# Attention scores: the scale moved into the queries, the maxima written negated, the mask added to the outer key blocks alone

## The chip, the cores and the metric

The kernel runs on one core of one Trainium2 chip, as one launch. The metric is the time of an execution on the device in microseconds (us); a lower number is better. The engines are called by their roles: TensorE (PE in the profile, its weight loads PEld), VectorE (DVE), ScalarE (ACT), GpSimd (POOL), and SyncE (SP), which issues the DMAs.

## What the kernel computes

Two blocks in a row on 512 tokens of width 1024. The first block (a convolution and pooling mixer, then a layer of 16384 experts looked up by key, then a gated embedding) takes the first 1700 us or so and isn't touched. The second block has two attention layers. The first, "a", is a windowed attention with 16 query heads on 4 key heads; its core in the reference is:

```
q = apply_rope(q, cos, sin);  k = apply_rope(k, cos, sin)        # the 512 tokens; the 256 context tokens are not rotated
near = jnp.abs(kj - BLOCK - qi) <= WINDOW                        # previous, own and next block of 128 keys
s_loc = jnp.einsum("bqhgd,bkhd->bhgqk", q, k).astype(F32) * scale    # scale = 64 ** -0.5
s_loc = jnp.where(m, s_loc, -jnp.inf)
s_ctx = jnp.einsum("bqhgd,bchd->bhgqc", q, kc).astype(F32) * scale
p = softmax_with_sink(jnp.concatenate([s_loc, s_ctx], axis=-1), sink_b)
...
sc = jnp.einsum("bqhgd,bkhd->bhgqk", qc, kc).astype(F32) * scale     # queries of the context
```

The second, "b", is a latent attention of 16 heads, in which each of the 512 queries attends to all 768 keys:

```
q = (rms_norm_2(cq, q_norm) @ w_uq);  rope on 32 of its 96 columns
s = (einsum(qn, kn) + einsum(qr, kr)) * scale                     # scale = 96 ** -0.5
p = jax.nn.softmax(s, axis=-1)
```

## The kernel before

Every engine has one list of instructions, written out in order in the functions `tensor`, `scalar`, `vector`, `gpsimd` and `sync`. Nothing reorders them. An engine runs ahead until a `wait_ge` on a semaphore that another engine (or an earlier instruction of its own) raises with `then_inc(*tick(...))`.

**Layer a.** The eight query units are projected one after the other (`on_both`, some 9 us each on TensorE). ScalarE copies the 512 token columns of a unit out of PSUM (L1203), TensorE multiplies them with the rotation matrix (L607), and VectorE finishes the rotation in three instructions (`rope`, L1704 to L1706). The 256 context columns come as two partial sums that VectorE adds up (`context_sum`, L1711). Then come 96 jobs. Job j is one block of 128 queries of one head; `a_job(j)` gives the query unit i (0 to 7), the half (which of the unit's two heads) and the block t (0 to 3 are the tokens, 4 and 5 the context). The two halves of one (i, t) are called a pair of jobs here, and there are 48 pairs, six to a unit. A half has its own PSUM area, `SC[half]`, and there is one of each, so that the scores of a pair can start only when both exponentials of the pair before have been read. A pair goes so:

- TensorE, `a_scores`: scores against the 256 context keys (L696); for t below 4 against the 256 or 384 near keys too (L701), onto which the mask is added by a matmul of the identity with the mask's columns, in the rounded fp32 type (L704). The mask holds 0 or -1e30.
- VectorE, `maxima`: for t = 0 a copy of the sink value (L1745) into the score area, for every job the row maximum (L1746) and its product with -scale (L1747).
- ScalarE, `exponents`: the exponential (L1212), which reads the scores, scales them, adds the bias from L1747 and sums the row.
- VectorE, `normalise`: the reciprocal of the sum (L1752) and the product (L1753).
- TensorE, `a_turn`: transposes (L718); ScalarE copies them out of PSUM (L1230 to L1236); a unit later TensorE weighs the values with them (L745, L747, L752), and VectorE multiplies by the gate (L1768).

TensorE's order is: scores of the next pair, some pieces of the weighing of the unit before, the transposes of this pair. With t = 0 the unit before is gated.

**Layer b.** 64 jobs, one block of 128 queries of one head each, eight to a pair of heads. The order on TensorE is: transposes (L726), scores of the job after next (L877, L878), a step of the next head pair's projection (L843, L848, L857, the rotation L607), a piece of the weighing (L888). ScalarE copies the projected queries out (L1339). VectorE's order is: normalise, in two of eight jobs the three rotation instructions, then `maxima`.

`far_sink` holds the sinks divided by the scale, since the scores in PSUM are unscaled:

```
sc, sm = SC[j % 2], small[:, j % 16, :]
step(("max", key, j), DVE.tensor_reduce(sm[:, 0:1], sc[:, lo:hi], AX.X, ALU.max))
DVE.tensor_scalar(sm[:, 1:2], sm[:, 0:1], -scale, None, ALU.mult).then_inc(*tick("maxed", (key, j)))
```

`step` puts a wait of VectorE on its own instruction behind it.

Of the kernel before, what the change touches and what calls it, by code (L numbers as in the profile page):

```python
# [8 lines left out]
F32 = mybir.dt.float32  # L9
F32R = mybir.dt.float32r  # L10
U32 = mybir.dt.uint32
AF = mybir.ActivationFunctionType
AX = mybir.AxisListType

P = 128
T = 512
# [110 lines left out]
def write(nc, d, known):  # L127
# [37 lines left out]
    gathered = nc.alloc_sbuf_tensor("gathered", [P, T], F32)[:, :]  # L165
    fin_gain = nc.alloc_sbuf_tensor("fin_gain", [P, KC], F32)
    small = nc.alloc_sbuf_tensor("small", [P, 16, 8], F32)
    far_sink = nc.alloc_sbuf_tensor("far_sink", [P, 16], F32)
    psum = nc.alloc_psum_tensor("psum", [P, 8 * T], F32)
    bank = [psum[:, b * T:(b + 1) * T] for b in range(8)]  # L170

# [211 lines left out]
    def tensor(PE):  # L383
# [299 lines left out]
        def a_scores(j):  # L683
            i, _, t = a_job(j)
            p = i % 2
            lo, tiles = a_tiles(t)
            both = [(SC[half], slice(64 * half, 64 * half + 64)) for half in range(2)]
            if j:
                PE.wait_ge(*at("exped", ("a", j - 2)))
                PE.wait_ge(*at("exped", ("a", j - 1)))  # L690
            else:
                PE.wait_ge(*at("mask_r", 0))
                for n in range(8):
                    PE.wait_ge(*at("roped", ("q", n)))
            for sc, rows in both:
                last = PE.matmul(sc[:, T:TC], qr[i][rows, t * P:(t + 1) * P], kt[rows, p, T:TC], start=True, stop=True)  # L696
            if t < NT:
                first = tiles[0]
                skip = (first - t + 1) * P
                for sc, rows in both:  # L700
                    PE.matmul(sc[:, lo:T], qr[i][rows, t * P:(t + 1) * P], kt[rows, p, first * P:(tiles[-3] + 1) * P],  # L701
                              start=True, stop=False)
                for sc, rows in both:
                    last = PE.matmul(sc[:, lo:T], mask_r[:, 3 * P:4 * P], mask_r[:, skip:skip + T - lo], start=False,  # L704
                                     stop=True)
            last.then_inc(*tick("scored", ("a", j)))


# [216 lines left out]
    def scalar(ACT):  # L925
# [271 lines left out]
        for i in range(8):  # L1197
            u = unit("a_q", i)
            high_weights(u + 1)
            if i == 0:  # L1200
                a_silu_ctx(7)
            ACT.wait_ge(*at("unit", u))
            ACT.activation(qr[i][:, 0:T], bank[2 * (i % 4)], AF.Copy).then_inc(*tick("qr", i))  # L1203
        ACT.activation(mask_r[:, 3 * P:4 * P], K("ident"), AF.Copy)
        ACT.activation(mask_r[:, 0:3 * P], K("mask"), AF.Copy).then_inc(*tick("mask_r", 0))

        def exponents(key, j, probs, lo, hi, scale, turned):
            sm = small[:, j % 16, :]
            ACT.wait_ge(*at("maxed", (key, j)))
            if turned >= 0:  # L1210
                ACT.wait_ge(*at("prob_turned", (key, turned)))
            ACT.activation(probs[j % len(probs)][:, 0:hi - lo], SC[j % 2][:, lo:hi], AF.Exp, bias=sm[:, 1:2], scale=scale,  # L1212
                           accum_out=sm[:, 2:3]).then_inc(*tick("exped", (key, j)))

        def a_exponents(j):
            exponents("a", j, prob, a_tiles(a_job(j)[2])[0], SINK + 1, A_SCALE, j // 2 * 2 - 4)

        def a_turn(j):
            i, half, t = a_job(j)
# [107 lines left out]
        def project(pair, step):  # L1327
# [8 lines left out]
            elif step % 2 == 0:  # L1336
                i = step // 2 - 1
                ACT.wait_ge(*at("q_up", (pair, i)))
                ACT.activation(q[head_rows[i], i, :], bank[7][head_rows[i], :], AF.Copy).then_inc(*tick("qh", (pair, i)))  # L1339

        def b_exponents(j):
            exponents("b", j, b_prob, 0, TC, B_SCALE, j - PROBS)

        def b_turn(j):
            pair, half, t = b_job(j)
# [34 lines left out]
    def vector(DVE):  # L1380
# [296 lines left out]
        first = VEC["g_final"][0]  # L1677
        step("fin_gain", DVE.tensor_tensor(fin_gain[:, :], ada[:, 0, 1, :, 0], vec[:, first:first + KC], ALU.mult))
        sinks = vec[:, VEC["sink"][0]:VEC["sink"][0] + 16]
        step("far_sink", DVE.tensor_scalar(far_sink[:, :], sinks, 1.0 / A_SCALE, None, ALU.mult))  # L1680


        DVE.wait_ge(*at("peer_added", 7))
# [48 lines left out]
        for i in range(8):  # L1732
            u = unit("a_q", i)
            low_weights(u + 1)
            if i:
                a_rope(("q", i - 1), qr[i - 1], 2 * ((i - 1) % 4))
            context_sum(u, 2 * (i % 4) + 1, qr[i][:, T:TC]).then_inc(*tick("qr_ctx", i))
        a_rope(("q", 7), qr[7], 6)
        DVE.wait_ge(*at("a_silu_ctx", 7))

        def maxima(key, j, lo, hi, scale, sink=None, scored=None):
            sc, sm = SC[j % 2], small[:, j % 16, :]
            DVE.wait_ge(*at("scored", (key, j if scored is None else scored)))
            if sink is not None:
                step(("sunk", j), DVE.tensor_copy(sc[:, SINK:SINK + 1], far_sink[:, sink:sink + 1]))  # L1745
            step(("max", key, j), DVE.tensor_reduce(sm[:, 0:1], sc[:, lo:hi], AX.X, ALU.max))  # L1746
            DVE.tensor_scalar(sm[:, 1:2], sm[:, 0:1], -scale, None, ALU.mult).then_inc(*tick("maxed", (key, j)))  # L1747

        def normalise(key, j, probs, n):
            pr, sm = probs[j % len(probs)], small[:, j % 16, :]  # L1750
# [3 lines left out]

        def a_maxima(j):
            i, half, t = a_job(j)
            maxima("a", j, a_tiles(t)[0], SINK + 1, A_SCALE, (i // 2) * 4 + 2 * (i % 2) + half if t == 0 else None,
                   j // 2 * 2)

        def a_normalise(j):  # L1760
# [84 lines left out]
                norm("b_cq")  # L1845

        def b_maxima(j):
            maxima("b", j, 0, TC, B_SCALE)

        def b_normalise(j):  # L1850
            normalise("b", j, b_prob, TC)
# [354 lines left out]
```

## Time and profile before

| | |
|---|---|
| median of 3 runs | 2546.21 us |
| lowest and highest | 2545.77, 2550.89 us |
| profiled execution, its own time | 2547.82 us |
| profiled execution, span | 2546.5 us |
| TensorE busy | 2365.4 us, 93% |
| VectorE busy | 1867.6 us, 73% |
| ScalarE busy | 1074.8 us, 42% |
| layer a, the jobs | 1775 to 1990 us from the span's start |
| layer b, projections of the head pairs and the jobs | 2165 to 2485 us |

Busy shares are means over the whole span. The two stretches of the attention jobs are some 535 us of it, and what is worth something there is read from the chain of work in them. The profiled execution lies 1.3 us over its span and 1.6 us over the median.

### The profile page before, as it was taken

How to read it: one execution, taken by the hardware profiler on the slowest of the kernel's cores; microseconds unless marked ns; L12 is line 12 of the kernel's file. 1: busy time of each engine (PE TensorE's matmuls, PEld its weight loads, DVE VectorE, ACT ScalarE, POOL GpSimd, SP SyncE). 2: the span in 40 equal slices, each digit the busy share in tenths (PEclk: the TensorE clock that was granted, in tenths of full speed). 3: DMA queues.
4: the chain of work that ended last, by engine and by line, in shares of the span. 5: the costliest groups of instructions: out<-in, count | busy, mean ns of one | idle time of the engine just before them, and what ended most of it. 6: DMA issues, size and time to landing. Idle time of an engine off the chain costs nothing.

```text
span 2546.5 us, 33616 instructions
## 1 busy us (share of the span) xinstructions
PE 2365.4 (93%) x12399; PEld 1986.8 (78%) x12399; DVE 1867.6 (73%) x3575; ACT 1074.8 (42%) x1910; POOL 623.0 (24%) x408
## 2 busy tenths in 40 slices
PE   7989999999999989999999998998778989899997
PEld 5768998999899989999999986786444767455555
DVE  7899898999999977878788875524676454155554
ACT  3332333333488843333333344321566333344452
POOL 4110367777722232323233302000000100000001
PEclk9999999999999999999999999999899999999999
DMA  6537456787788999999999941111000112100001
GB/s 246 188 134 252 163 191 223 248 249 251 246 318 322 326 366 358 367 357 363 327 368 367 365 153 59 58 58 50 1 1 1 50 42 99 36 19 19 10 1 67
DMA packets 162227, 465.95 MB, mean 183 GB/s; under 512 B 15504, under 2 KB 72976, under 8 KB 159632
## 3 DMA queue, kind: packets, MB, share of 16 engines
q1 hardware_dynamic: 100368, 304.40, 34.1%
q0 software_dynamic: 36864, 134.23, 14.8%
q10 hardware_dynamic: 24832, 25.17, 3.0%
q8 instruction: 99, 1.62, 0.3%
q14 instruction: 64, 0.52, 0.1%
HBM read 411.31 MB, written 52.43 MB: 182 GB/s over the span
## 4 chain that ended last, share of the span: by engine, by line
PE 70%; DVE 17%; ACT 4%; DMA 4%; issue 3%; POOL 2%; DVEq 0%; ACTq 0%
PE psum L572 6%; PE psum L574 6%; PE psum L573 6%; PE psum L428 5%; PE psum L430 5%; PE psum L429 5%; PE psum L436 4%; PE psum L438 4%; PE psum L437 4%; PE psum L545 3%; PE psum L857 2%; DMA arena<-hidden 2%; PE psum L454 2%; POOL weights_low L1948 2%; DVE small L1746 2%
## 5 line engine op out<-in xcount | busy, mean ns | idle before, releaser
L934 ACT ACTIVATE weights_high<-arena 128x1024 fp32r<-128x1024 f32 x355 | 374.8, 1056 | 439.7 <-PE psum L574 303.6
L1387 DVE TENSOR_TENSOR weights_low<-arena,weights_high 128x1024 fp32r<-128x1024 f32 x266 | 334.6, 1258 | 217.7 <-ACT weights_high L934 208.8
L436 PE MATMUL psum<-x_high,weights_high 128*128 128x384 f32 x1024 | 352.3, 344 | 28.8 <-POOL weights_low L1948 19.5
L572 PE MATMUL psum<-hidden_high,weights_high 128*128 128x384 f32 x1024 | 344.9, 337 | 10.2 <-DVE hidden_low L1649 8.0
L438 PE MATMUL psum<-x_high,weights_low 128*128 128x384 f32 x1024 | 344.4, 336 | 0.0
L437 PE MATMUL psum<-x_low,weights_high 128*128 128x384 f32 x1024 | 344.2, 336 | 0.0
L573 PE MATMUL psum<-hidden_low,weights_high 128*128 128x384 f32 x1024 | 343.4, 335 | 0.0
L574 PE MATMUL psum<-hidden_high,weights_low 128*128 128x384 f32 x1024 | 343.2, 335 | 0.0
L428 PE MATMUL psum<-x_high,weights_high 128*128 128x512 f32 (+1 forms) x696 | 277.1, 398 | 24.7 <-DVE weights_low L1387 19.9
L1948 POOL TENSOR_TENSOR weights_low<-arena,weights_high 128x1024 fp32r<-128x1024 f32 x89 | 227.1, 2552 | 201.3 <-ACT weights_high L934 200.8
L429 PE MATMUL psum<-x_low,weights_high 128*128 128x512 f32 (+1 forms) x696 | 271.7, 390 | 0.0
L430 PE MATMUL psum<-x_high,weights_low 128*128 128x512 f32 (+1 forms) x696 | 271.6, 390 | 0.0
L1942 POOL DMA_INDIRECT arena<-in_v_rows,arena x128 | 152.4, 1191 | 376.2 <-DVE arena L1600 340.8
L436 PEld LDWEIGHTS psum<-x_high,weights_high 128*128 128x128 f32 x1024 | 193.7, 189 | 45.6 <-issue 42.1
L572 PEld LDWEIGHTS psum<-hidden_high,weights_high 128*128 128x128 f32 x1024 | 193.1, 189 | 12.7 <-DVE weights_low L1387 9.7
L1942 POOL DMA_INDIRECT arena<-in_u_rows,arena x128 | 152.1, 1188 | 195.2 <-DVE arena L1584 180.8
L1584 DVE SCALAR_TENSOR_TENSOR arena<-arena 128x1024 f32<-128x1024 f32 x128 | 181.8, 1422 | 17.4 <-DMA arena<-in_u_rows,arena 17.2
L437 PEld LDWEIGHTS psum<-x_low,weights_high 128*128 128x128 f32 x1024 | 193.8, 189 | 0.0
L438 PEld LDWEIGHTS psum<-x_high,weights_low 128*128 128x128 f32 x1024 | 193.4, 189 | 0.0
L573 PEld LDWEIGHTS psum<-hidden_low,weights_high 128*128 128x128 f32 x1024 | 193.3, 189 | 0.0
L574 PEld LDWEIGHTS psum<-hidden_high,weights_low 128*128 128x128 f32 x1024 | 193.3, 189 | 0.0
L1212 ACT ACTIVATE arena<-psum,small 128x768 f32<-128x768 f32 (+3 forms) x160 | 120.3, 752 | 168.0 <-DVE small L1747 166.6
(238 smaller groups left out, 4182.8 us busy)
## 6 DMA issues: line engine op xcount, KB each, us to landing
arena<-in_stream SPq DMA_DIRECT2D x227, 512.0 KB
arena<-in_v_rows SPq DMA_DIRECT2D x128, 512.0 KB
arena<-in_ada_w SPq DMA_DIRECT2D x48, 512.0 KB, 3.3
hidden<-arena SPq DMA_DIRECT2D x128, 192.0 KB
router<-arena SPq DMA_DIRECT2D x12, 2048.0 KB
arena<-hidden SPq DMA_DIRECT2D x128, 192.0 KB
arena<-router ACTq DMA_DIRECT2D x16, 1536.0 KB
arena<-in_pair_w SPq DMA_DIRECT2D x8, 576.0 KB, 3.9
```

Source lines behind the costliest of these rows:

```text
L428: PE.matmul(out, wh[w][:, k, 0:m], rh[:, k, 0:n], start=k == order[0], stop=False)
L429: PE.matmul(out, wh[w][:, k, 0:m], rl[:, k, 0:n], start=False, stop=False)
L430: last = PE.matmul(out, wl[w][:, k, 0:m], rh[:, k, 0:n], start=False, stop=k == order[ks - 1])
L436: PE.matmul(bank[b][:, 0:N], wh[u % 2][:, k, :], xh[:, k, PICKED:T], start=k == 0, stop=False)
L437: PE.matmul(bank[b][:, 0:N], wh[u % 2][:, k, :], xl[:, k, PICKED:T], start=False, stop=False)
L438: last = PE.matmul(bank[b][:, 0:N], wl[u % 2][:, k, :], xh[:, k, PICKED:T], start=False, stop=k == KC - 1)
L572: PE.matmul(out, wh[w][:, n, :], hh[:, r, :], start=e == 0, stop=False)
L573: PE.matmul(out, wh[w][:, n, :], hl[:, r, :], start=False, stop=False)
L574: last = PE.matmul(out, wl[w][:, n, :], hh[:, r, :], start=False, stop=e == KEYS - 1)
L934: ACT.activation(wh[u % 2], slots[u % RING], AF.Copy).then_inc(*tick("weights_high", u))
L1387: DVE.tensor_tensor(wl[u % 2], slots[u % RING], wh[u % 2].bitcast(F32), ALU.subtract).then_inc(*tick("weights", u))
L1942: POOL.indirect_dma_start(rows[j % ROW_RING], None, d[f"{table}_rows"], bass.IndirectOffsetOnAxis(ap=chosen[:, entry:entry + 1].bitcast(U3 ...
```

## The change

Four edits, in both layers unless said otherwise.

1. The scale moves from the exponential into the queries. ScalarE's copies out of PSUM (L1203 in layer a, L1339 in layer b) get `scale=`. In layer a the context columns don't pass ScalarE, so VectorE multiplies them in SBUF, one instruction of 128x256 for each of the eight query units, behind a wait on its own sum.
2. The row maximum is written with `negate=True` directly where the exponential reads its bias. The product with -scale (L1747) is gone.
3. In layer a the mask is added to the outer blocks of keys alone: for t = 1 and 2 to the previous and the next block by one matmul with two runs of 128 columns, for t = 0 and 3 to the one outer block. The middle block's mask is all zeros.
4. The sinks are copied from the vectors as they are; `far_sink` and its one instruction are gone.

```diff
             if t < NT:
                 first = tiles[0]
-                skip = (first - t + 1) * P
...
+                sides = [0] * (t > 0) + [2] * (t < NT - 1)
                 for sc, rows in both:
-                    last = PE.matmul(sc[:, lo:T], mask_r[:, 3 * P:4 * P], mask_r[:, skip:skip + T - lo], start=False,
-                                     stop=True)
+                    if len(sides) == 2:
+                        out = sc[:, lo:T].rearrange("p (n c) -> p n c", c=P)[:, 0:3:2, :]
+                        cut = mask_r[:, 0:3 * P].rearrange("p (n c) -> p n c", c=P)[:, 0:3:2, :]
+                    elif sides == [2]:
+                        out, cut = sc[:, T - P:T], mask_r[:, 2 * P:3 * P]
+                    else:
+                        out, cut = sc[:, lo:lo + P], mask_r[:, 0:P]
+                    last = PE.matmul(out, mask_r[:, 3 * P:4 * P], cut, start=False, stop=True)
...
-            ACT.activation(qr[i][:, 0:T], bank[2 * (i % 4)], AF.Copy).then_inc(*tick("qr", i))
+            ACT.activation(qr[i][:, 0:T], bank[2 * (i % 4)], AF.Copy, scale=A_SCALE).then_inc(*tick("qr", i))
...
-            ACT.activation(probs[j % len(probs)][:, 0:hi - lo], SC[j % 2][:, lo:hi], AF.Exp, bias=sm[:, 1:2], scale=scale,
+            ACT.activation(probs[j % len(probs)][:, 0:hi - lo], SC[j % 2][:, lo:hi], AF.Exp, bias=sm[:, 1:2],
...
-                ACT.activation(q[head_rows[i], i, :], bank[7][head_rows[i], :], AF.Copy).then_inc(*tick("qh", (pair, i)))
+                ACT.activation(q[head_rows[i], i, :], bank[7][head_rows[i], :], AF.Copy,
+                               scale=B_SCALE).then_inc(*tick("qh", (pair, i)))
...
-            context_sum(u, 2 * (i % 4) + 1, qr[i][:, T:TC]).then_inc(*tick("qr_ctx", i))
+            context_sum(u, 2 * (i % 4) + 1, qr[i][:, T:TC]).then_inc(*tick("qr_ctx_sum", i))
+            DVE.wait_ge(*at("qr_ctx_sum", i))
+            DVE.tensor_scalar(qr[i][:, T:TC], qr[i][:, T:TC], A_SCALE, None, ALU.mult).then_inc(*tick("qr_ctx", i))
...
-                step(("sunk", j), DVE.tensor_copy(sc[:, SINK:SINK + 1], far_sink[:, sink:sink + 1]))
-            step(("max", key, j), DVE.tensor_reduce(sm[:, 0:1], sc[:, lo:hi], AX.X, ALU.max))
-            DVE.tensor_scalar(sm[:, 1:2], sm[:, 0:1], -scale, None, ALU.mult).then_inc(*tick("maxed", (key, j)))
+                step(("sunk", j), DVE.tensor_copy(sc[:, SINK:SINK + 1], sinks[:, sink:sink + 1]))
+            DVE.tensor_reduce(sm[:, 1:2], sc[:, lo:hi], AX.X, ALU.max, negate=True).then_inc(*tick("maxed", (key, j)))
```

VectorE's list, at the last query unit and the first pair of jobs of layer a, before the change (arena is the query unit, psum the scores, small the maxima and sums):

```order
L1711 TENSOR_REDUCE arena<-psum 128x256
L1704 TENSOR_TENSOR arena<-psum,con 128x512
L1705 TENSOR_TENSOR arena<-arena,con 128x512
L1706 TENSOR_TENSOR arena<-arena 128x512
L1745 COPY psum<-far_sink 128x1
L1746 TENSOR_REDUCE small<-psum 128x1
L1747 TENSOR_SCALAR small<-small 128x1
L1745 COPY psum<-far_sink 128x1
L1746 TENSOR_REDUCE small<-psum 128x1
L1747 TENSOR_SCALAR small<-small 128x1
```

The same place of VectorE's list in the changed kernel:

```order
L1717 TENSOR_REDUCE arena<-psum 128x256
L1745 TENSOR_SCALAR arena<-arena 128x256
L1710 TENSOR_TENSOR arena<-psum,con 128x512
L1711 TENSOR_TENSOR arena<-arena,con 128x512
L1712 TENSOR_TENSOR arena<-arena 128x512
L1753 COPY psum<-vec 128x1
L1754 TENSOR_REDUCE small<-psum 128x1
L1753 COPY psum<-vec 128x1
L1754 TENSOR_REDUCE small<-psum 128x1
```

One instruction of 128x256 is new ahead of the last rotation, and the two small products are gone.

## Rows read from the trace of the kernel before

**Rows 1.** Windows: stretch, length, PE, PEld, DVE, ACT, POOL busy, clock, DMA share, GB/s.

```profile
1775.00:1990.00 215.00, 166.41 (x997) 100.56 (x998) 142.38 (x422) 124.36 (x391) 0.00 (x0) 0.92 0.00 1
2165.00:2485.00 320.00, 301.59 (x1328) 162.39 (x1326) 153.31 (x312) 142.60 (x256) 0.00 (x0) 0.99 0.05 17
```

**Rows 2.** Waits in 1775 to 1990: us in total, times, longest.

```profile
ACT arena L1212 <- DVE small L1747: 75.8, 41, 6.3
```

**Rows 3.** Chain that ended last, 1690 to 2090: start, us, what.

```profile
1892.11 1.87 PE psum L745 x8
...
1916.33 1.87 PE psum L745 x8
...
1966.41 1.87 PE psum L745 x8
```

**Rows 4.** Timeline of one pair with t = 0: start, us, idle before.

```profile
1882.46 0.69 DVE L1746 TENSOR_REDUCE small<-psum 128x1 f32<-128x513 f32 x1
1883.18 0.15 DVE L1747 TENSOR_SCALAR small<-small 128x1 f32<-128x1 f32 x1
1883.26 0.15 DVE L1745 COPY psum<-far_sink 128x1 f32<-128x1 f32 x1
1883.37 0.69 ACT L1212 ACTIVATE arena<-psum,small 128x513 f32<-128x513 f32 x1 [2.31 <-DVE small L1747]
...
1884.36 0.69 ACT L1212 ACTIVATE arena<-psum,small 128x513 f32<-128x513 f32 x1 [0.20 <-DVE small L1747]
```

**Rows 5.** Timeline of the next pair, t = 1.

```profile
1887.22 0.83 DVE L1746 TENSOR_REDUCE small<-psum 128x1 f32<-128x641 f32 x1 [1.03 <-PE psum L704]
...
1888.26 0.80 ACT L1212 ACTIVATE arena<-psum,small 128x641 f32<-128x641 f32 x1 [2.58 <-DVE small L1747]
...
1889.18 0.80 ACT L1212 ACTIVATE arena<-psum,small 128x641 f32<-128x641 f32 x1
```

**Rows 6.** Timeline, t = 2 to 5 of the unit before.

```profile
1870.92 0.70 PE L696 MATMUL psum<-arena 64*128 64x256 f32 x4
...
1875.15 0.70 PE L696 MATMUL psum<-arena 64*128 64x256 f32 x4 [0.19 <-ACT arena L1212]
...
1878.03 0.70 PE L696 MATMUL psum<-arena 64*128 64x256 f32 x4
...
1878.94 0.41 ACT L1233 ACTIVATE arena<-psum 128x256 f32<-128x256 f32 x1
...
1879.43 0.48 ACT L1212 ACTIVATE arena<-psum,small 128x257 f32<-128x257 f32 x1
```

**Rows 7.** Mask matmuls: a pair of 256, a pair of 384 columns.

```profile
1881.72 0.51 PE L704 MATMUL psum<-mask_rounded 128*128 128x256 f32 x2
...
1891.49 0.62 PE L704 MATMUL psum<-mask_rounded 128*128 128x384 f32 x2
```

**Rows 8.** Last query unit, and a product of 128x256 on VectorE.

```profile
1772.53 0.69 DVE L1711 TENSOR_REDUCE arena<-psum 128x256 f32<-128x512 f32 x1
1773.13 0.68 DVE L1704 TENSOR_TENSOR arena<-psum,con 128x512 f32<-128x512 f32 x1
...
1877.33 0.35 DVE L1753 TENSOR_SCALAR arena<-arena,small 128x256 f32<-128x256 f32 x1
```

**Rows 9.** Timeline, TensorE in layer b: after a rotation, the last pair.

```profile
2316.98 0.88 PE L726 MATMUL psum<-con,arena 128*128 128x128 f32 x6 [1.02 <-DVE arena L1753]
...
2317.70 1.02 PE L877 MATMUL psum<-arena 128*128 128x512 f32 x2
...
2462.17 0.87 PE L726 MATMUL psum<-con,arena 128*128 128x128 f32 x6 [0.58 <-DVE arena L1753]
...
2479.76 0.87 PE L726 MATMUL psum<-con,arena 128*128 128x128 f32 x6 [0.86 <-DVE arena L1753]
```

**Rows 10.** Two stretches around a drop of the clock, columns as in rows 1.

```profile
1936.60:1940.00 3.40, 1.33 (x9) 0.82 (x9) 2.41 (x7) 2.86 (x8) 0.00 (x0) 1.00 0.00 0
1940.00:1943.40 3.40, 3.40 (x11) 1.07 (x10) 2.41 (x6) 1.47 (x3) 0.00 (x0) 0.52 0.00 0
```

More of the change, by code:

```diff
@@ L167, in write @@
     small = nc.alloc_sbuf_tensor("small", [P, 16, 8], F32)
-    far_sink = nc.alloc_sbuf_tensor("far_sink", [P, 16], F32)
     psum = nc.alloc_psum_tensor("psum", [P, 8 * T], F32)
@@ L1202, in scalar, with exponents @@
             ACT.wait_ge(*at("unit", u))
-            ACT.activation(qr[i][:, 0:T], bank[2 * (i % 4)], AF.Copy).then_inc(*tick("qr", i))
+            ACT.activation(qr[i][:, 0:T], bank[2 * (i % 4)], AF.Copy, scale=A_SCALE).then_inc(*tick("qr", i))
         ACT.activation(mask_r[:, 3 * P:4 * P], K("ident"), AF.Copy)
         ACT.activation(mask_r[:, 0:3 * P], K("mask"), AF.Copy).then_inc(*tick("mask_r", 0))
-        def exponents(key, j, probs, lo, hi, scale, turned):
+        def exponents(key, j, probs, lo, hi, turned):
             sm = small[:, j % 16, :]
@@ L1211, in exponents @@
                 ACT.wait_ge(*at("prob_turned", (key, turned)))
-            ACT.activation(probs[j % len(probs)][:, 0:hi - lo], SC[j % 2][:, lo:hi], AF.Exp, bias=sm[:, 1:2], scale=scale,
+            ACT.activation(probs[j % len(probs)][:, 0:hi - lo], SC[j % 2][:, lo:hi], AF.Exp, bias=sm[:, 1:2],
                            accum_out=sm[:, 2:3]).then_inc(*tick("exped", (key, j)))
         def a_exponents(j):
-            exponents("a", j, prob, a_tiles(a_job(j)[2])[0], SINK + 1, A_SCALE, j // 2 * 2 - 4)
+            exponents("a", j, prob, a_tiles(a_job(j)[2])[0], SINK + 1, j // 2 * 2 - 4)
         def a_turn(j):
@@ L1338, in project @@
                 ACT.wait_ge(*at("q_up", (pair, i)))
-                ACT.activation(q[head_rows[i], i, :], bank[7][head_rows[i], :], AF.Copy).then_inc(*tick("qh", (pair, i)))
+                ACT.activation(q[head_rows[i], i, :], bank[7][head_rows[i], :], AF.Copy,
+                               scale=B_SCALE).then_inc(*tick("qh", (pair, i)))
         def b_exponents(j):
-            exponents("b", j, b_prob, 0, TC, B_SCALE, j - PROBS)
+            exponents("b", j, b_prob, 0, TC, j - PROBS)
         def b_turn(j):
@@ L1679, in vector @@
         sinks = vec[:, VEC["sink"][0]:VEC["sink"][0] + 16]
-        step("far_sink", DVE.tensor_scalar(far_sink[:, :], sinks, 1.0 / A_SCALE, None, ALU.mult))
         DVE.wait_ge(*at("peer_added", 7))
@@ L1736, in vector, with maxima @@
                 a_rope(("q", i - 1), qr[i - 1], 2 * ((i - 1) % 4))
-            context_sum(u, 2 * (i % 4) + 1, qr[i][:, T:TC]).then_inc(*tick("qr_ctx", i))
+            context_sum(u, 2 * (i % 4) + 1, qr[i][:, T:TC]).then_inc(*tick("qr_ctx_sum", i))
+            DVE.wait_ge(*at("qr_ctx_sum", i))
+            DVE.tensor_scalar(qr[i][:, T:TC], qr[i][:, T:TC], A_SCALE, None, ALU.mult).then_inc(*tick("qr_ctx", i))
         a_rope(("q", 7), qr[7], 6)
         DVE.wait_ge(*at("a_silu_ctx", 7))
-        def maxima(key, j, lo, hi, scale, sink=None, scored=None):
+        def maxima(key, j, lo, hi, sink=None, scored=None):
             sc, sm = SC[j % 2], small[:, j % 16, :]
@@ L1756, in a_maxima @@
             i, half, t = a_job(j)
-            maxima("a", j, a_tiles(t)[0], SINK + 1, A_SCALE, (i // 2) * 4 + 2 * (i % 2) + half if t == 0 else None,
+            maxima("a", j, a_tiles(t)[0], SINK + 1, (i // 2) * 4 + 2 * (i % 2) + half if t == 0 else None,
                    j // 2 * 2)
@@ L1847, in b_maxima @@
         def b_maxima(j):
-            maxima("b", j, 0, TC, B_SCALE)
+            maxima("b", j, 0, TC)
         def b_normalise(j):
```

## The prediction, made blind

> **What bounds the kernel now.** I read the page first: TensorE is busy 93% of the span, so only a stretch in which it is not can give anything to a change on VectorE. The busy times by stretch come next [rows 1]. In the jobs of layer a TensorE works 166 of 215 us, in layer b 302 of 320. The waits of layer a say who keeps whom: the exponential waited 75.8 us for the small product L1747 [rows 2]. It is the last link of a loop, since a half's score area exists once: scores, mask, maximum, product, exponential, next scores. The chain view shows the period: the weighing L745 is on it at 1892.11 and 1916.33, one query unit of six pairs in 24.2 us [rows 3]. So a link counts where the next scores wait for ScalarE, and costs nothing where TensorE's own list is behind.
>
> **The two things that shorten a pair.**
>
> Mask. A pair of 384-column mask matmuls takes 0.62 us, one of 256 columns 0.51 [rows 7]: 0.11 us for 256 columns, or 0.43 ns a column. Each matmul loses 128 columns, from 384 to two runs of 128 (t = 1, 2) or from 256 to 128 (t = 0, 3). If columns stay at that price, every pair with t below 4 gets 0.11 us ahead of its maximum. No row shows a rounded matmul under 256 columns, or one that writes PSUM in two runs; the bounds are below.
>
> Product. With t = 1 the maximum starts at 1887.22, lasts 0.83, and the exponential starts 1.04 us after the maximum's start [rows 5]. From a product's end to the exponential is 0.04 us (1883.18 + 0.15 to 1883.37 [rows 4]). I take the same for a maximum that signals itself: 0.83 + 0.04 = 0.87, a saving of 0.17 to 0.18. I assume that the negated maximum lasts as long as the plain one. The second exponential starts 0.92 after the first [rows 5], which is ScalarE's own time for one, and the second maximum is ready by then too, so the pair gains 0.18 once and not twice.
>
> With t = 0 the sink copy stands between. Now the second exponential starts 1.90 after the first maximum's start (1884.36 less 1882.46 [rows 4]). After: maximum 0.69, the copy starts 0.07 before its end (as it now does before the product's end), second maximum 0.20 after the copy, 0.69 long, then 0.04: 1.55. Saving 0.35.
>
> **Pair by pair in a unit.**
> - t = 0: 0.11 + 0.35 = 0.46.
> - t = 1: 0.11 + 0.18 = 0.29.
> - t = 2: the next scores, at 1870.92, start right behind the transposes with no idle time of TensorE, so its own list is the limit [rows 6]. The mask's 0.11 shortens that list; I put 0.05 of slack between the two limits, an estimate between the 0 that the row shows and the 0.18 of a full gain: 0.16.
> - t = 3: the next scores waited 0.19 for ScalarE [rows 6], which the 0.18 fit into: 0.29.
> - t = 4: no mask, and the scores at 1878.03 follow TensorE's list without idle [rows 6]: 0.
> - t = 5: the first exponential starts at 1879.43, but ScalarE's copy before it ends at 1879.35 [rows 6]: 0.07.
>
> That is 1.27 us a unit, 10.2 for eight. In unit 0 there is nothing to weigh, so t = 2 gets its full 0.29, and TensorE runs at half clock for part of it, where 256 columns take about 0.2 instead of 0.11; I add 0.6. After the last unit two products less stand ahead of the gate: 0.1.
>
> **What is added.** The context product, eight times. VectorE takes 0.35 us for 128x256 [rows 8] and waits for its own sum. For units 0 to 6 TensorE's next unit hides it: VectorE's list for a unit is the sum, three rotation instructions of 0.7 us and one for low weights, well under the unit's 9 us, and what stands behind the product are low weights that TensorE needs only after that unit. If that cover went, it would cost 0.4 each, 2.8 in all. At the last unit it is on the path: the sum at 1772.53, then the rotation at 1773.13, 0.60 apart because nothing waits [rows 8]. After: 0.69 + 0.04 + 0.35 - 0.07 = 1.01, so 0.4 us later for the first scores. The scale on ScalarE's copies I take as free, since the exponential carried a scale in the same kind of instruction. If each copy grew by a tenth, only those on the path would show, the last of layer a and two for each head pair of b, under 1 us together. `far_sink`'s one instruction lies before layer a, behind other waits: nothing. Layer a: 10.2 + 0.6 + 0.1 - 0.4 = 10.5.
>
> **Layer b.** TensorE's list is the bound nearly everywhere. Once for each head pair the two rotations hold VectorE back and the transposes wait 1.02 us [rows 9]. The path there is rotation, maximum, product, exponential, normalise, transposes, so 0.19 comes off; six such places and a start alike: 1.3. In the last head pair nothing is projected and the loop over VectorE and ScalarE takes over: TensorE waited 0.58 and 0.86 [rows 9], with 0.23 between them. A loop without the product is 0.19 shorter, but TensorE's list then becomes the bound again, so I give it 0.19 at its rotation, 0.38 to the first, 0.23 to the second and 0.2 to the last: 1.0. Layer b: 2.3.
>
> **Sum.** 10.5 + 2.3 = 12.8 us. The profiled execution took 2547.8, so its like takes 2535.0; the median lies 1.6 below it: 2533.4, said as 2533.5, or 0.5% faster. A measurement of this kernel tells about 0.2% (5.1 us) from no change.
>
> **A rule that speaks against it.** Rows 7 show contiguous output only. The Trainium skill ("PSUM — Partial Sum Buffer", Specifications) says that any non-contiguous access pattern slows matmuls significantly, and gives no figure. By that rule the two runs of 128 columns would cost more than the 384 columns that they replace; by the rows' price they cost 0.11 less a pair. No run here shows it yet. I lean to the rows, because each run is 128 neighbours long.
>
> **Rivals.**
>
> *A. The mask matmuls get dear per column.* The upper bound is the full-precision matmul: 512 columns in 1.02 us [rows 9], 2.0 ns a column. The fixed part of a mask pair is 0.51 - 512 x 0.43 ns = 0.29. (a) Only the 128-column ones: 0.29 + 0.51 = 0.80 for a pair instead of 0.40, at t = 0 and 3: 16 x 0.4 = 6.4 us, 2539.9. (b) Only the ones in two runs: 0.29 + 1.02 = 1.31 instead of 0.51, 16 x 0.8 = 12.8 us, 2546.3, no change; this is also the skill's rule as a mechanism. (c) Both: 19.2 us, 2552.7, **slower**. Over 12,288 mask columns it decides at 12.8 / 12,288 = 1.04 ns a column more, about 1.5 ns. For it speaks that no row has these shapes; against it that contiguous rounded matmuls of 256 and 384 columns differ by plain streaming. Chances: (a) 12%, (b) 6%, (c) 3%.
>
> *B. The clock takes some of it.* The mean granted clock of the stretch is 0.92 [rows 1]: it falls to 0.52 (of 2.4 GHz, so nearly all at 1.2) in a stretch that follows one with TensorE busy 1.33 of 3.40 us [rows 10]. Two units that hold this drop take 1966.41 - 1916.33 = 50.1 us instead of 48.4 [rows 3], 1.6 us for one drop. The change takes some work from TensorE and more waiting, and shifts every pair, so drops may fall elsewhere. Three more of them: 2538.5. Two or three fewer: 2529.5. Chance of giving back 4 us or more: 7%; of a gain beyond 16 us: 4%.
>
> *C. The product was hidden.* If the maximum that signals itself took 0.15 us longer to be seen, only the masks would be left (32 pairs x 0.11 = 3.5 and 0.3) against the 0.4: about 2543, within the noise. Against it: instruction ends and the next engine's start are 0.04 apart everywhere in rows 4. Chance 3%.
>
> **How the numbers follow.** The forecast itself, 2530 to 2537, has 65%. The range 2528 to 2542 takes in rivals A(a) and B and leaves out A(b), A(c), C and the far tail, some 15%. Faster by over 0.2%: the forecast, nearly all of A(a) and B: 0.88. Within 0.2%: A(b), C and a bit of A(a) and B: 0.08. Slower: A(c) and what I have missed: 0.04.
>
> **What the changed profile would show.** L1747 gone, and the exponential 0.87 after the start of a 641-column maximum; a negated maximum of 0.83; mask pairs of 0.40 (one block) and 0.51 (two blocks); a unit in about 22.95 us from L745 to L745; first scores 0.4 us later against the last rotation's matmul; in layer b the seven waits of 1.02 down to 0.83, and the last pair's down by 0.8 together. Wrong would make it: mask pairs at 0.8 or more; unit periods that differ from one another by over 1 us with drops of the clock; ScalarE as the one that is late for t = 0 to 3, since then the 0.18 would be lost.

## The result, and the profile after

| | before | after |
|---|---|---|
| median | 2548.39 us (4 runs) | 2523.81 us (4 runs) |
| lowest and highest | 2545.77, 2550.89 us | 2522.62, 2527.90 us |
| profiled execution, own time | 2547.82 us | 2527.90 us |

The ratio is 0.9909, with a 95% interval of 0.9895 to 0.9924, so 0.9% faster. The median before is that of four runs here, one more than in the table ahead of the prediction. The forecast was 2533.5, with a range of 2528 to 2542; the measured 2523.81 lies 4.2 us below that range. The direction was right, and the forecast gain was about half of the gain that came (12.7 of 24.6 us). A second, longer measurement gave 0.992 (0.990 to 0.9941).

The busy times of layer a's jobs, columns as in rows 1, from the first scores to the weighing of the last unit: first the kernel before, then the changed one. The last line is layer b of the changed kernel.

```profile
1775.29:1981.56 206.27, 160.35 (x960) 97.27 (x961) 139.67 (x414) 122.39 (x384) 0.00 (x0) 0.92 0.00 1
```

```profile
1773.20:1963.05 189.85, 152.46 (x960) 94.17 (x961) 124.96 (x318) 117.03 (x384) 0.00 (x0) 0.94 0.00 1
...
2150.00:2465.00 315.00, 297.86 (x1312) 159.55 (x1310) 145.53 (x249) 142.63 (x257) 0.00 (x0) 0.99 0.04 13
```

Layer a's jobs are 16.4 us shorter. TensorE's waiting in them fell by 8.5 us (from 45.9 to 37.4) and its busy time by 7.9 us, with the same number of matmuls: the mask matmuls have fewer columns, and more of the others ran at the higher clock (0.94 against 0.92). To see where, take a point that occurs once a unit, the start of the weighing, from the chain that ended last:

```profile
1879.10 1.87 PE psum L751 x8
...
1901.76 1.87 PE psum L751 x8
...
1924.41 1.87 PE psum L751 x8
...
1948.51 1.97 PE psum L751 x8
```

A unit takes 22.66 us (1901.76 less 1879.10), where it took 24.2 [rows 3] and I had forecast 22.95. The last one here took 24.10: a drop of the clock. The pair with t = 0 of the changed kernel, timeline, against [rows 4]:

```profile
1892.37 0.44 PE L711 MATMUL psum<-mask_rounded 128*128 128x128 f32 x2
...
1893.04 0.69 DVE L1754 TENSOR_REDUCE small<-psum 128x1 f32<-128x513 f32 x1
1893.65 0.15 DVE L1753 COPY psum<-vec 128x1 f32<-128x1 f32 x1
...
1893.77 0.69 ACT L1218 ACTIVATE arena<-psum,small 128x513 f32<-128x513 f32 x1 [2.06 <-DVE small L1754]
1893.84 0.69 DVE L1754 TENSOR_REDUCE small<-psum 128x1 f32<-128x513 f32 x1
...
1894.57 0.69 ACT L1218 ACTIVATE arena<-psum,small 128x513 f32<-128x513 f32 x1
```

From the first maximum's start to the second exponential's is 1.53 us; 1.90 before, 1.55 forecast. The negated maximum is as long as the plain one, 0.69. The next pair, t = 1, against [rows 5]:

```profile
1896.77 0.51 PE L711 MATMUL psum<-mask_rounded 128*128 128x256 f32 x2
...
1897.31 1.56 DVE L1754 TENSOR_REDUCE small<-psum 128x1 f32<-128x641 f32 x2 [0.92 <-PE psum L711]
1898.17 0.80 ACT L1218 ACTIVATE arena<-psum,small 128x641 f32<-128x641 f32 x1 [2.28 <-DVE small L1754]
1898.86 0.19 ACT L1218 ACTIVATION_READ_ACCUMULATOR arena<-psum,small 128x1 f32 x1
1898.95 0.79 ACT L1218 ACTIVATE arena<-psum,small 128x641 f32<-128x641 f32 x1
```

Two things are to be seen. The mask matmuls with two runs of 128 columns take 0.51 us a pair, the same as one run of 256 did [rows 7], so two runs cost nothing that the records show. And the second exponential starts 0.78 us after the first, not 0.92: it even starts 0.10 before the reading of the accumulator ends. The same overlap shows at t = 5, against [rows 6]:

```profile
1889.84 0.41 ACT L1239 ACTIVATE arena<-psum 128x256 f32<-128x256 f32 x1
1890.14 0.48 ACT L1218 ACTIVATE arena<-psum,small 128x257 f32<-128x257 f32 x1
```

The copy ends at 1890.25 and the exponential has started at 1890.14.

Ahead of the first scores the added product stands between the sum and the rotation, 0.94 us apart instead of 0.60 [rows 8]:

```profile
1770.11 0.69 DVE L1717 TENSOR_REDUCE arena<-psum 128x256 f32<-128x512 f32 x1
1770.84 0.29 DVE L1745 TENSOR_SCALAR arena<-arena 128x256 f32<-128x256 f32 x1
1771.05 0.68 DVE L1710 TENSOR_TENSOR arena<-psum,con 128x512 f32<-128x512 f32 x1
```

Layer b, TensorE's timeline, against [rows 9]:

```profile
2297.82 0.88 PE L732 MATMUL psum<-con,arena 128*128 128x128 f32 x6 [0.83 <-DVE arena L1760]
...
2441.87 0.87 PE L732 MATMUL psum<-con,arena 128*128 128x128 f32 x6 [0.21 <-DVE arena L1760]
...
2459.04 0.87 PE L732 MATMUL psum<-con,arena 128*128 128x128 f32 x6 [0.85 <-DVE arena L1760]
```

Seven waits of 1.02 are 0.83 now, as forecast. In the last head pair the first wait fell from 0.58 to 0.21 (0.38 less forecast). The second, of 0.23, is gone, and the transposes there start 0.38 earlier (0.23 forecast). The last stayed at 0.85, where 0.2 less was forecast.

**Where the first unit went.** From the first scores to the first weighing (unit 0 and two pairs more) it took 42.8 us before and 36.3 after, 6.5 less, where eight pairs at the new speed explain less than 3. The windows over this stretch, before and then after, tell of the clock (the column ahead of the last two):

```profile
1775.30:1818.20 42.90, 29.80 (x132) 20.27 (x134) 23.21 (x68) 19.50 (x60) 0.00 (x0) 0.67 0.00 1
```

```profile
1773.20:1809.50 36.30, 24.22 (x130) 16.73 (x130) 20.78 (x52) 18.74 (x60) 0.00 (x0) 0.79 0.00 1
```

So a part of the gain is a higher clock. The experiments had to tell the parts from one another.

### The profile page after: what moved, and what is told of

The parts are those of the page before. It is cut to its first block, busy times and chain, and to the rows that moved or that the text cites. A ratio compares the mean times of both kernels' runs of the same rounds, so it can differ in the third digit from the quotient of the medians.

```text
span 2526.6 us, 33463 instructions
## 1 busy us (share of the span) xinstructions
PE 2357.1 (93%) x12399; PEld 1983.8 (79%) x12399; DVE 1845.5 (73%) x3422; ACT 1069.9 (42%) x1910; POOL 625.5 (25%) x408
## 4 chain that ended last, share of the span: by engine, by line
PE 70%; DVE 14%; DMA 5%; ACT 4%; issue 4%; POOL 2%; DVEq 0%; ACTq 0%
PE psum L427 6%; PE psum L429 5%; PE psum L428 5%; PE psum L571 5%; PE psum L573 5%; PE psum L572 5%; PE psum L435 4%; PE psum L437 4%; PE psum L436 4%; DMA arena<-hidden 4%; PE psum L544 3%; PE psum L863 2%; PE psum L453 2%; POOL weights_low L1955 2%; PE psum L883 2%
## 5 line engine op out<-in xcount | busy, mean ns | idle before, releaser
L435 PEld LDWEIGHTS psum<-x_high,weights_high 128*128 128x128 f32 x1024 | 193.5, 189 | 42.8 <-issue 39.3
L1052 ACT ACTIVATE arena<-psum 128x384 f32<-128x384 f32 x128 | 62.6, 489 | 295.9 <-PE psum L437 274.6
```

Of the source, the lines that this page charges most:

```text
L435: PE.matmul(bank[b][:, 0:N], wh[u % 2][:, k, :], xh[:, k, PICKED:T], start=k == 0, stop=False)
```

## The experiments

Two theories stood against each other on the pairs. Theory 1: ScalarE can start the next instruction before the one ahead has quite ended, and what kept the second exponential at 0.92 us was the second product. The rival is my forecast's reading: 0.92 is ScalarE's own time. On the first unit and on the longer units: the clock, or something else in the change.

The table has, for each traced execution, the start of the rotation right behind the last projection, the time from there to the first scores, from those to the first weighing, the period of a unit where the clock holds, the number of the six later periods that are over 0.5 us longer than that, and layer b from its first transposes to its last. All are differences of starts in the timelines. The rotation in the first column is that of the seventh query unit; the expectations call it the eighth's, which follows 0.86 us later in the traces of both kernels. Ahead of it lie the untouched first block and the projections, which have seven of the eight added products; the rotations there follow one another 9.11 us apart before and after, so these products are hidden.

| kernel | rotation at | to scores | first unit | period | longer | layer b |
|---|---|---|---|---|---|---|
| before | 1769.4 | 5.87 | 42.81 | 24.23 | 2 | 261.6 |
| before again | 1763.6 | 5.86 | 40.86 | 24.23 | 2 | 263.4 |
| mask alone | 1766.2 | 5.87 | 42.37 | 23.87 | 0 | 263.3 |
| scale and maximum alone | 1768.9 | 6.20 | 38.08 | 23.0 | 2 | 261.2 |
| after | 1767.0 | 6.19 | 36.33 | 22.66 | 2 | 259.5 |
| after again | 1770.4 | 6.19 | 36.32 | 22.65 | 2 | 259.5 |
| product at the first job | 1766.9 | 6.20 | 38.51 | 23.37 | 2 | 259.5 |
| product at the second job | 1767.8 | 6.20 | 36.59 | 23.12 | 3 | 259.5 |
| layer a only | 1769.6 | 6.20 | 38.45 | 22.65 | 2 | 261.7 |
| after, start filled | 1770.5 | 6.19 | 33.18 | 22.65 | 1 | 259.5 |
| after, waits filled | 1766.9 | 6.19 | 36.37 | 22.65 | 0 | 259.5 |
| after, both | 1771.2 | 6.19 | 33.36 | 22.65 | 0 | 261.2 |
| before, both | 1761.0 | 5.87 | 39.65 | 24.24 | 0 | 261.7 |
| after, filled more | 1769.1 | 6.19 | 32.62 | 22.65 | 0 | 259.5 |
| before, filled more | 1770.4 | 5.86 | 36.79 | 24.23 | 0 | 263.3 |

**Before again.** No edit.

> The kernel before, unchanged, for the spread between executions. My theory of the missing 12 us is that some 6 us of the layer-a stretch were mis-sized (see the runs beside this one) and the rest is spread between executions and drops of TensorE's clock. Theory 1 expects a ratio of 1.000 within 0.002, the jobs of layer a in the same 24.2 us a unit, and the point where the eighth rotation's matmul starts (1769.4 us in the profile before) to move by 2 us or more from execution to execution. The rival, that the kernel before is stable there and the change moved it, expects this point within 0.5 us of 1769.4.

Ratio 1.0015 (0.9994 to 1.0036). Units of 24.23, and the rotation at 1763.6, 5.9 us earlier than in the first trace of the same kernel. So the 1770 us ahead of layer a's jobs scatter by several us, and the 2.4 us that the first two traces differ by there are within that scatter. Over all traces of the table the rotation starts between 1761.0 and 1771.2, in the kernels with both old products between 1761.0 and 1770.4; no gain shows there.

**The mask edit alone.**

```diff
+                sides = [0] * (t > 0) + [2] * (t < NT - 1)
...
+                    last = PE.matmul(out, mask_r[:, 3 * P:4 * P], cut, start=False, stop=True)
```

> The kernel before with the mask edit alone. By the rows, 0.11 us for each of four pairs in a unit, and where TensorE's list is the limit too: a unit in 24.2 - 0.44 = 23.8 us, 3.5 us in all, ratio 0.9986. If the two edits helped each other (the missing gain came from an interaction), the mask alone gives under 0.3 us a unit or the product alone well under 1.1. If drops of the clock are what the change mostly moved, the unit's period says 23.8 but the ratio is off from that by 2 us or more.

Ratio 0.9978 (0.9964 to 0.9992); period 23.87, so 0.36 us a unit, 2.9 us in eight, against 0.44 expected. From scores to scores the pairs with two outer blocks (t = 1, 2) gained the 0.11 of the forecast, and those with one (t = 0, 3) only 0.07, since their mask pair takes 0.44 us and not 0.40. Its trace has no drop in the later units, one more reason to go by periods and not by totals.

**Scale and negated maximum alone.** The changed kernel with the old line `last = PE.matmul(sc[:, lo:T], mask_r[:, 3 * P:4 * P], mask_r[:, skip:skip + T - lo], start=False, stop=True)`.

> The changed kernel with the mask added to all blocks as before, so only the scale and the negated maximum. Theory 1: the second exponential was held by the second product and not by ScalarE, so a pair gains 0.18 twice where ScalarE is the limit: a unit in 24.22 - (1.57 - 0.44) = 23.1 us; layer a some 9 us shorter, layer b 2.2 us, ratio about 0.9955. The rival, my forecast's reading (0.92 us is ScalarE's own time for an exponential), expects 23.4 us a unit and 0.9965.

Ratio 0.9949 (0.9932 to 0.9965); period 23.0 where the clock holds, 1.23 us a unit. Theory 1 said 23.1, the rival 23.4; the interval of the ratio holds both forecasts, so the period decides. By pair these two edits gave 0.37, 0.33, 0, 0.26, 0 and 0.25 for t = 0 to 5: at t = 2, where TensorE's list is the limit, only the mask counts. The two parts, 0.36 and 1.23, make 1.59, and both together gave 1.58: they add up, so no interaction hides a gain.

**After again.** No edit.

> The changed kernel again, on this chip beside the others. Theory 1: 22.66 us a unit as in its first profile, with zero to three units longer by 1.4 us where the clock drops, and a ratio between 0.990 and 0.993; the trace says whether the stretch before layer a (matmul of the eighth rotation at 1767.0 us) is the same or moves from execution to execution. The rival, that the change made the stretch ahead of layer a faster, expects it at 1767.0 within 0.5 us again.

Ratio 0.992 (0.990 to 0.9941). The jobs of layer a repeat the first trace within 0.05 us, drops of the clock in the same units included, though the rotation starts 3.4 us later.

**The product back at one job of a pair.** `product at the first job` has the lines below with 0, `at the second job` with 1.

```diff
+            if key == "a" and j % 2 == 0:
+                step(("max", key, j), DVE.tensor_reduce(sm[:, 0:1], sc[:, lo:hi], AX.X, ALU.max))
+                DVE.tensor_scalar(sm[:, 1:2], sm[:, 0:1], -1.0, None, ALU.mult).then_inc(*tick("maxed", (key, j)))
+            else:
```

> The changed kernel with the small product put back in layer a for the first job of each pair alone (the product is by -1, behind a plain maximum). Theory 1 (ScalarE starts a next exponential 0.78 us after one of 641 columns, whatever held it at 0.92 before): the first exponential comes 0.18 us later and takes the second with it, 0.10 to 0.18 a pair where ScalarE is the limit, so t = 1 4.48 + 0.18 = 4.66 us and the unit 22.65 + 0.6 to 0.8. The rival (0.92 is ScalarE's own) expects the same here, 0.18 a pair; the run beside this one tells them apart.

> The changed kernel with the small product put back for the second job of each pair alone. Theory 1: the first exponential at 0.87 from the first maximum, the second at 1.79 instead of 1.65, held by the product: 0.14 us more for t = 1 (4.62 us) and a unit 0.4 to 0.7 us longer than 22.65. The rival (ScalarE's own 0.92) expects the second at 0.87 + 0.92 = 1.79 with or without this product, so the unit stays at 22.65 within 0.1 us.

Each of the two was executed once, for its trace. With the product at the first job the period is 23.37, 0.71 us more (0.6 to 0.8 expected), and t = 1 takes 4.67 (4.66 expected). With the product at the second job the clock drops in every other unit, and a drop lengthens the weighing period of the next unit too, by 0.1 to 0.2. So its period is read from the scores of t = 0 in a unit without a drop, TensorE's timeline:

```profile
1896.51 0.70 PE L695 MATMUL psum<-arena 64*128 64x256 f32 x4 [0.40 <-ACT arena L1218]
...
1919.63 0.70 PE L695 MATMUL psum<-arena 64*128 64x256 f32 x4 [0.40 <-ACT arena L1218]
```

That is 23.12 us, 0.47 more (0.4 to 0.7 expected). The two together make 1.18, close to the 1.23 of both at once. The second is the decisive one: the rival expected nothing. Its timeline at t = 1, where the next scores come 4.63 us after these (4.62 expected), with the second job's product:

```profile
1903.55 0.80 ACT L1218 ACTIVATE arena<-psum,small 128x641 f32<-128x641 f32 x1 [2.27 <-DVE small L1758]
1904.25 0.19 ACT L1218 ACTIVATION_READ_ACCUMULATOR arena<-psum,small 128x1 f32 x1
1904.29 0.15 DVE L1756 TENSOR_SCALAR small<-small 128x1 f32<-128x1 f32 x1
...
1904.47 0.80 ACT L1218 ACTIVATE arena<-psum,small 128x641 f32<-128x641 f32 x1
```

0.92 us apart again, and no idle bracket on the last row, as in [rows 5]. The reading of the accumulator and the product both end at 1904.44, and the exponential starts at 1904.47: no wait is marked on so small a gap, and yet the product sets the start, for without it the two exponentials are 0.78 apart. My forecast's reading fell here. The kernel before has the same coincidence, its second product ahead of the exponential at 1889.18 of [rows 5]:

```profile
1889.00 0.15 DVE L1747 TENSOR_SCALAR small<-small 128x1 f32<-128x1 f32 x1
```

**Start filled.** Work without use for TensorE ahead of the first scores, in the changed kernel; what it writes is never read.

```diff
+        PE.wait_ge(*at("roped", ("q", 5)))
+        for n in range(4):
+            PE.matmul(bank[0], K("ident"), con[:, 0:T], start=True, stop=True)
         a_scores(0)
```

> The changed kernel with four 128x512 full-precision matmuls without use (into PSUM bank 0) ahead of the first scores, where TensorE waits 4.2 us for the last rotation. Theory 1: the clock is at its lower level for the first unit because TensorE was idle before it; with work there the first unit takes 36.3 less 3 to 5 us, the rest is the same, ratio about 0.9905. The rival (the clock is low because the first unit itself is thin) expects the low clock to come back within the first two pairs and 0 to 1.5 us in all. If the matmuls end after the last rotation they cost up to 1 us.

Ratio 0.9902 (0.987 to 0.9935). The first unit fell from 36.3 to 33.18 with the same instructions in it, and the first scores came no later (6.19). The clock over the first unit was 0.95 instead of 0.79:

```profile
1776.70:1809.90 33.20, 20.69 (x132) 14.56 (x132) 20.78 (x52) 18.78 (x60) 0.00 (x0) 0.95 0.00 1
```

**Waits filled.** Rounded matmuls without use in TensorE's two long waits of each unit.

```diff
             a_turn(j)
+            for n in range({5: 4, 0: 8}.get(t, 0) if j + 4 < A_JOBS else 0):
+                PE.matmul(bank[7][:, 0:3 * P], mask_r[:, 3 * P:4 * P], mask_r[:, 0:3 * P], start=True, stop=True)
```

> The changed kernel with rounded matmuls without use (384 columns, into bank 7, which nobody reads then) in TensorE's waits of each unit: four behind the transposes of t = 5, eight behind those of t = 0. They are meant to fill 0.65 of 1.08 us and 1.3 of 1.83 us. Theory 1: no unit is longer than 22.7 us any more (two were 24.1, 2.9 us in all), the first unit is shorter by up to 3 us, ratio 0.990 to 0.991. The rival (drops depend on something other than how busy TensorE is): units of 24.1 stay. If the filling reaches into the scores' start, all units get longer by the overhang, seen as a unit over 22.8.

Ratio 0.9905 (0.9878 to 0.9932). All six later periods are 22.65: the two of 24.1 are gone. The first unit stayed at 36.37, so the part that expected it to shorten was wrong. The clock was already low when it began, so the eight matmuls behind t = 0 took 2.40 us and held the next scores: that pair was 0.99 us longer than without filling, and the fifth 0.50. The third was 1.44 shorter at the higher clock, which about makes up for it.

**Both fillings,** in the changed kernel and in the one before.

> The changed kernel with both fillings: four full-precision matmuls without use ahead of the first scores and the rounded ones in the waits of each unit. If the two effects measured singly add up, the first unit takes 33.2 us, every other 22.65, and the jobs of layer a are 6 us shorter than in the changed kernel; ratio 0.988 to 0.990. The rival, that the first unit's drop was already cured by chance and the two overlap, gives 3 us or less.

> The kernel before with the same two fillings, to compare the two kernels at the full clock throughout. Theory 1: units of 24.23 us without exception, a first unit near 33.2 + 1.6 + 0.9 + 0.3 = 36.0 us (six pairs with t = 2 at its full gain, and two more), the jobs of layer a 201 us or so, ratio about 0.998; against the filled changed kernel 1.58 a unit and nothing else, so what the change won beyond 12.6 us in layer a was the clock. The rival: the first unit stays above 39 us, so the change shortened it by something else.

The changed kernel: ratio 0.9902 (0.988 to 0.9924), first unit 33.36, all others 22.65; the jobs of layer a are 6.1 us shorter than without filling (6 expected), so the two effects add. The kernel before: 0.9966 (0.9954 to 0.9977), all later units 24.24, but the first one 39.65 and not 36.0. That is the number that the rival had asked for. But the clock over it was only 0.83 (against 0.95 in the changed kernel), and I had filled only two kinds of its waits. So the question stayed open, and more filling had to answer it.

**Layer a only.** The changed kernel with layer b's scale in the exponential and its product kept.

> The changed kernel with layer b as before (scale in the exponential, product kept). Both my forecast and theory 1: layer a as in the changed kernel (22.65 us a unit), the transposes of layer b from the first to the last in 261.6 us instead of 259.5, so 2.1 us, if the clock doesn't drop in it (263.4 if it does).

Layer b takes 261.65 us from the first transposes to the last instead of 259.51: 2.1 us, with layer a at 22.65 a unit.

**Filled more.** In both kernels as above, and in unit 0 behind the first scores and the transposes.

```diff
+        def fill(b, n):
+            for _ in range(n):
+                PE.matmul(bank[b][:, 0:3 * P], mask_r[:, 3 * P:4 * P], mask_r[:, 0:3 * P], start=True, stop=True)
...
         a_scores(0)
+        fill(6, 12)
...
             a_turn(j)
+            if i == 0:
+                fill(6, (8, 8, 6, 2, 0, 4)[t])
+            elif j + 4 < A_JOBS:
+                fill(7, {5: 4, 0: 8}.get(t, 0))
```

> The changed kernel with matmuls without use ahead of the first scores, behind them, behind every transposes of unit 0 except t = 4, and in the two long waits of the other units. If the first unit is now at the full clock throughout it takes about 33 us (it was 33.2 and 33.4 with less filling, since it was nearly at the full clock already), all others 22.65.

> The kernel before with the same filling. Theory 1 (what the change won in the first unit beyond 2.9 us was the clock): the first unit takes 33.2 + 1.58 + 0.89 + 0.4 = 36.0 us within 0.5 at a granted clock of 1.0, against 42.8 and 40.9 without filling and 39.7 with less. The rival (something else in the change shortened the first unit): it stays above 38 us although the granted clock is 1.0 throughout.

The windows over the first unit and 130 us behind it, the changed kernel and the one before, both filled:

```profile
1775.30:1807.90 32.60, 27.54 (x180) 21.29 (x180) 20.78 (x52) 18.89 (x60) 0.00 (x0) 1.00 0.00 1
1807.90:1937.90 130.00, 119.34 (x784) 76.06 (x785) 90.69 (x233) 85.12 (x280) 0.00 (x0) 1.00 0.00 1
```

```profile
1776.20:1813.00 36.80, 29.69 (x179) 22.59 (x179) 23.21 (x68) 19.55 (x60) 0.00 (x0) 0.95 0.00 1
1813.00:1943.00 130.00, 114.85 (x737) 72.17 (x738) 94.65 (x279) 83.18 (x261) 0.00 (x0) 1.00 0.00 1
```

The changed kernel was at the full clock throughout, the one before in all but one pair. That pair, from the timeline of its scores:

```profile
1805.01 0.91 PE L696 MATMUL psum<-arena 64*128 64x256 f32 x4 [1.91 <-ACT arena L1224]
1805.64 1.55 PE L701 MATMUL psum<-arena 64*128 64x384 f32 x4
...
1811.17 0.70 PE L696 MATMUL psum<-arena 64*128 64x256 f32 x4 [0.36 <-ACT arena L1224]
```

It took 6.16 us, where a pair with t = 1 takes 4.93 (1885.28 to 1890.21 in the first trace): 1.2 us for the drop. 36.79 - 1.2 = 35.6, within the 0.5 of 36.0, and 2.9 us over the 32.62 of the changed kernel, just what I had reckoned for the pairs' own gains. So what the first unit won beyond that in the first pair of traces was the clock. Ratios: 0.9889 (0.986 to 0.9919) for the changed kernel, 0.9956 (0.9935 to 0.9977) for the one before. The filled changed kernel is the fastest by its median ratio; its trace has 183.1 us from the first scores to the last unit's weighing against 189.9 without filling. By time alone the two intervals overlap, so those 6.8 us are shown by the trace and not by the timing.

The timing does say something on the two filled kernels against each other. Filled more, their medians are 2538.25 and 2523.24, 15.0 us apart on the same chip (16.8 by their means); with both fillings 17.7 (15.9). Unfilled, "before again" and "after again" are 20.2 apart (21.6). So part of what the change wins seems to go when both kernels are filled, as it would if that part is the clock. With single executions of these kernels between 2518 and 2564 us that is a hint and no proof.

## Why the prediction was off

**Right.** The direction. A negated maximum costs what a plain one does, and signals 0.04 us after its end: 0.86 from its start to the exponential's, 0.87 forecast. t = 0 gained as said (1.53 against 1.55). t = 4 gained nothing (2.88 us between its scores and the next, before and after). The added product was hidden seven times and cost 0.3 once (0.4 forecast). Layer b gave 2.1 us (2.3 forecast): 0.19 in each of seven places, then 0.38 twice in the last head pair. There the forecast had 0.38, 0.23 and another 0.2, so two small errors nearly cancel. The scale on ScalarE's copies cost nothing: 0.60 us as before.

**The step that failed** was "0.92 after the first, which is ScalarE's own time for one", and with it the term "0.07" for t = 5. I read the distance of two starts as the length of work because no wait was marked between them. It was a coincidence: the second product ended 0.03 ahead of the start, and ScalarE would have been ready 0.14 earlier. The starts of the scores of the six pairs in the two traces:

| t | forecast | before to after | gain |
|---|---|---|---|
| 0 | 0.46 | 4.62 to 4.18 | 0.44 |
| 1 | 0.29 | 4.93 to 4.49 | 0.45 |
| 2 | 0.16 | 4.94 to 4.82 | 0.11 |
| 3 | 0.29 | 4.23 to 3.90 | 0.33 |
| 4 | 0 | 2.88 to 2.88 | 0 |
| 5 | 0.07 | 2.63 to 2.38 | 0.25 |

That is 1.58 against 1.27 a unit, 2.5 us in eight. Both products weigh on the path, as the two one-sided kernels show (0.71 and 0.47), and not the first alone. Two smaller terms were off the other way: the mask's 0.11 at t = 0 and 3 was 0.07, and the 0.05 given to the product at t = 2 was 0. By itself this step doesn't account for the miss: with 2.5 us more gain the forecast is 2531.0, still 7.2 us above the measured time.

**The second term** is the clock, and by size it is the larger. The forecast put it at a part of 0.6 us in the first unit, and the rivals had it on the wrong side: 7% for the clock taking 4 us or more, 4% for a gain beyond 16 us. In the first pair of traces the jobs of layer a are 16.4 us shorter (206.3 to 189.9), in the pair filled more 14.4, of which 1.2 is the drop: 13.1 at one clock, 0.3 less for the later start. So 3.3 us came from the clock there, all in the first unit. The second pair of traces says 0.8 by the same sum (203.7 to 189.8, so 13.9), since "before again" had a shorter first unit (40.86). And "layer a only", with the instructions of the changed kernel in layer a, has 38.45 where that has 36.33. So the clock's share moves by 2 us and more between executions, and two traces don't give its size.

**What stays open.** Layer a at one clock (12.8 after the later start) and layer b (2.1) make 15 us, which the experiments show. The clock in the two traced pairs adds 3.3 and 0.8, so 18 and 16; the timed ratios say 19 to 27 and 15 to 25 us.

For the rest the granted clocks of all executions give a hint. In 83 executions of the kernel before, beside the experiments, the mean clock is 0.9788, and the longer ones have the lower clock: 2563.0 us in the mean at 0.972 and 0.973 (4 executions), 2546.0 at 0.979 (30), 2542.6 at 0.983 (5). The traced ones of that kernel stand at 0.980 and 0.982, above that mean; the ten executions of the changed kernel at 0.9825. An estimate: a straight line through the 83 has 1.8 us for 0.001 of the clock, so the 0.0037 between the kernels is 6.7 us, and with the 15 that makes some 21.6, where the means differ by 21.8. That is a correlation over four chips (1.0 to 2.7 us for 0.001 on single ones) and no experiment. The smaller distances of the filled pairs point the same way; where in the kernel the untraced executions lose the clock stays open.

**The other rivals.** Dear mask matmuls (A) are refuted: a pair takes 0.44 with 128 columns and 0.51 with two runs. The rule of the Trainium skill ("PSUM — Partial Sum Buffer", Specifications), that any non-contiguous pattern slows matmuls significantly, does not show for two runs of 128 neighbours: 0.51 us against 0.51 for 256 in one run [rows 7], and in "mask alone" the scores of a pair with two runs follow 0.11 us earlier (4.93 to 4.82 us). The measurement decides. C is refuted by the 0.04 in the changed kernel.

## What to carry to other kernels

When the gap between the end of one record on an engine and the start of the next is too small to be marked as a wait, look whether another engine's signal ends in the same place before calling it the engine's own time; take the engine's own pace from a place where nothing can hold it. A latency loop with little work for TensorE pays for its clock too: in the traces, matmuls without use in waits that exist anyway gave 3.1 us in one unit and took away every long period, though no timed ratio tells this filling from none. And compare kernels by the period of a repeated unit at one clock, since totals of two executions differed here by more than an edit was worth; take it from a unit whose neighbour has no drop either. When such totals are forecast all the same, give the clock a term of its own that can go both ways.

## What was not expected of the hardware

- An instruction of ScalarE starts up to 0.11 us before the record of the one ahead ends (the copy at 1889.84 and the exponential at 1890.14): 0.78 between the starts of two exponentials of 641 columns, whose 0.80 and the accumulator's 0.19 would not fit; on VectorE two maxima take 1.56 for 2 x 0.82.
- In both traces of the changed kernel TensorE had been idle for 4.2 us ahead of the first scores, and the first 15 us from there ran at a granted clock of 0.50; with four matmuls put into the wait they ran at 0.88, and the first unit took 33.2 instead of 36.3 us. The length of the low stretch isn't fixed: in "before again" 6.8 us at 0.50, begun 1.2 us behind the first scores, were followed by some at 1.00.
- Drops fell in the same two units in both executions of the changed kernel (24.09 and 24.10 us, then 24.10 twice), although the stretch ahead had moved by 3.4 us; in the kernel before only one of two units was the same. From the scores of t = 0 to those of the next unit a later unit with one drop is 1.5 to 1.6 us longer (24.19 against 22.65 after, 25.85 against 24.23 before); by the starts of the weighing a part of this can fall on the next period.
